# Low halves of the expert weights written over the pieces they are formed from

## The reference

```python
logits = (hf @ w_router + b_router).astype(jnp.float32)
top_vals, top_idx = lax.top_k(logits, TOP_EXPERTS)
gates = jax.nn.softmax(top_vals, axis=-1)
...
def expert_block(args):
    tok, g, e = args
    xb = h_pad[tok]
    gu = xb @ w_gu[e] + b_gu[e]
    glu = jnp.minimum(gu[:, :D_EXPERT], SWIGLU_LIMIT)
    lin = jnp.clip(gu[:, D_EXPERT:], -SWIGLU_LIMIT, SWIGLU_LIMIT)
    act = glu * jax.nn.sigmoid(SWIGLU_ALPHA * glu) * (lin + 1.0)
    return (act @ w_down[e] + b_down[e]) * g[:, None].astype(h.dtype)
```

## Time and profile before

| | us |
|---|---|
| median of 3 runs | 1449.99 |
| lowest and highest | 1448.58, 1451.81 |
| the profiled execution | 1450.44 |
| its span, first to last instruction | 1448.7 |

### The profile page before, as it was taken

How to read it: one execution, slowest core, us unless ns; L and a number is a source line. 1 busy time by engine, 2 the same in 40 slices (tenths; PEclk the granted TensorE clock), 3 DMA queues, 4 the chain that set the end, 5 groups by cost and what they waited for, 6 DMA issues and landing times. The chain is left out here.

```text
span 1448.7 us, 18694 instructions
## 1 busy us (share of the span) xinstructions
PE 1369.2 (95%) x6693; PEld 1112.4 (77%) x6696; DVE 1261.1 (87%) x1314; ACT 1117.4 (77%) x1221; POOL 220.0 (15%) x138
## 2 busy tenths in 40 slices
PE   6999878999999999999999999999999999999995
PEld 5887766786788878778777788787787787787884
DVE  5799778548899899999999899989999999998994
ACT  5666554455788898988988788988889888888783
POOL 1222000011111111211202011111111111030100
PEclk9999979999999999999999999999999999999998
DMA  5522011158999999999999999999999999999991
GB/s 152 148 71 73 30 59 45 45 193 307 332 382 376 371 379 398 405 389 396 395 401 386 395 374 401 406 388 393 387 389 397 381 391 379 400 391 385 378 391 30
DMA packets 85926, 448.52 MB, mean 310 GB/s; under 512 B 18496, under 2 KB 23616, under 8 KB 36608
## 3 DMA queue, kind: packets, MB, share of 16 engines
q1 hardware_dynamic: 73424, 428.32, 75.0%
q0 software_dynamic: 9792, 18.90, 5.4%
q10 hardware_dynamic: 2608, 0.01, 0.1%
HBM read 440.89 MB, written 23.07 MB: 320 GB/s over the span
## 5 line engine op out<-in xcount | busy, mean ns | idle before, releaser
L840 DVE TENSOR_TENSOR whl<-wraw,whl 128x2048 fp32r<-128x2048 f32 x384 | 864.3, 2286 | 70.8 <-ACT whl L835 68.6
L835 ACT ACTIVATE whl<-wraw 128x2048 fp32r<-128x2048 f32 x384 | 728.5, 1917 | 143.3 <-PE ps L2163 95.6
L2163 PE MATMUL ps<-whl,xT 128*128 128x512 f32 x2768 | 660.5, 394 | 8.4 <-DVE whl L840 3.9
L2163 PEld LDWEIGHTS ps<-whl,xT 128*128 128x128 f32 x2768 | 514.0, 188 | 124.8 <-DVE whl L840 14.8
L2163 PE MATMUL ps<-whl,aT 128*128 128x512 f32 x1312 | 314.1, 396 | 14.2 <-DVE whl L840 14.2
L2163 PEld LDWEIGHTS ps<-whl,aT 128*128 128x128 f32 x1312 | 245.2, 189 | 68.5 <-DVE whl L840 18.4
L1029 POOL DMA_INDIRECT out_dram<-ysb,idx x32 | 86.0, 2688 | 623.2 <-ACT ysb L1344 623.2
L1020 POOL DMA_INDIRECT xg<-h_rows,idx x32 | 84.7, 2648 | 258.8 <-DVE idx L1794 253.7
L1906 PE MATMUL ps<-W,HT 128*128 128x512 f32 (+1 forms) x184 | 72.1, 392 | 5.4 <-DVE W L612 4.4
L1908 PE MATMUL ps<-W,HT 128*128 128x512 f32 (+1 forms) x184 | 68.9, 375 | 0.0
L1907 PE MATMUL ps<-W,HT 128*128 128x512 f32 (+1 forms) x184 | 68.8, 374 | 0.0
(11 more groups left out here) (296 smaller groups left out, 1400.8 us busy)
## 6 DMA issues: line engine op xcount, KB each, us to landing
wraw<-in_w_gu_dram SPq DMA_DIRECT2D x256, 1024.0 KB, 15.8
wraw<-in_w_down_dram SPq DMA_DIRECT2D x128, 1024.0 KB, 14.5
WR<-in_w_in_dram SPq DMA_DIRECT2D x20, 512.0 KB, 3.7
WR<-in_w_o_dram SPq DMA_DIRECT2D x8, 512.0 KB, 3.7
xs<-in_x_dram SPq DMA_DIRECT2D x4, 512.0 KB, 7.7
WR<-in_x_dram SPq DMA_DIRECT2D x4, 512.0 KB, 3.8
out_dram<-WR SPq DMA_DIRECT2D x4, 512.0 KB, 3.3
h_rows<-WR SPq DMA_DIRECT2D x4, 512.0 KB, 2.6
```

The source lines that it names most:

```text
L835: act.activation(whl[:, n % HL, 0, :], wraw[n % RAW], ACT.Copy).then_inc(chunk_hi, 1)
L840: eng.tensor_tensor(whl[:, n % HL, 1, :], wraw[n % RAW], whl[:, n % HL, 0, :].bitcast(F32), ALU.subtract).then_inc(chunk_lo, 1)
L2163: ins = pe.matmul(bank, a[x_][j], w[:, b, j, 512 * q:512 * q + 512], start=c == NG and j == 0 and n == 0, stop=last and j == nj - 1 and n ...
```

## The change

The raw slots become ten and the upper halves six. The low half of a piece is written into its own raw slot, over the raw values, and read there by TensorE. The space is the same: six raw slots, two more where the first pair of halves lay, six upper halves of 8 KB behind them. As a raw slot now holds the low half until TensorE has used it, load n waits for `chunk_used` of piece n - 10, and upper half n for that of piece n - 6. The first eight loads are issued where they were; load 8 waits for the first upper half (after which `W1` is free), since slots 8 and 9 lie on `W1`. The number of landings of a slot in a round is no longer the same for each slot, as 384 isn't a multiple of 10, and `split_hi` counts them. `EARLY` keeps the first four upper halves where they stood.

```diff
--- before.py
+++ after.py
@@ -273,7 +273,8 @@
 NG, ND = KD, KD // 2
 NCH = NG + ND
 PER_ROUND = NCH * E
-RAW, HL = 8, 4
+RAW, HL = 10, 6
+PREFETCH, EARLY = 8, 4
 LEAD = 2
 GLU_TOP = LIMIT / (1.0 + math.exp(-ALPHA * LIMIT))
 DENSE_AT = [(0, 3), (0, NG), (1, 1), (1, 5)]
@@ -359,10 +360,12 @@
         x1T = xres.rearrange("p (k n) -> p k n", k=KD)
         GF = rel.rearrange("p a b -> p (a b)")
 
-        whl = place("whl", [P, HL, 2, 2048], F32R, offset=base + 49152)
+        whi = place("whi", [P, HL, 2048], F32R, offset=base + 65536)
         o_qb = base + 49152 + 65536
-        wraw = [place(f"wraw{s}", [P, 2048], F32, offset=base + 8192 * s if s < 6 else o_qb + 66560 + 8192 * (s - 6))
-                for s in range(RAW)]
+        slot_at = [base + 8192 * s if s < 6 else o_qb + 66560 + 8192 * (s - 6) if s < 8 else base + 8192 * (s - 2)
+                   for s in range(RAW)]
+        wraw = [place(f"wraw{s}", [P, 2048], F32, offset=slot_at[s]) for s in range(RAW)]
+        wlo = [place(f"wlo{s}", [P, 2048], F32R, offset=slot_at[s]) for s in range(RAW)]
         bgs = place("bgs", [P, 3072], F32R, offset=o_qb)
         bg_raw = place("bg_raw", [P, 3072], F32, offset=o_qb + 12288)
         aT = place("aT", [P, 2, KD, P], F32R, offset=o_qb + 16384)
@@ -823,22 +826,21 @@
         def load_chunk(eng, r, e, c, at_=None):
             n = chunk_no(e, c)
             w = wraw[n % RAW]
-            after(eng, chunk_lo, PER_ROUND * r + n - RAW + 1)
+            after(eng, chunk_used, PER_ROUND * r + max(n - RAW + 1, 0))
             eng.dma_start(w if c < NG else w.rearrange("p (j n) -> p j n", j=2),
                           chunk_src(e, c, at_)) \
                .then_inc(landed[n % RAW], 16)
 
         def split_hi(act, r, e, c):
             n = chunk_no(e, c)
-            act.wait_ge(landed[n % RAW], 16 * (PER_ROUND // RAW * r + n // RAW + 1))
+            act.wait_ge(landed[n % RAW], 16 * (len(range(n % RAW, PER_ROUND, RAW)) * r + n // RAW + 1))
             after(act, chunk_used, PER_ROUND * r + n - HL + 1)
-            act.activation(whl[:, n % HL, 0, :], wraw[n % RAW], ACT.Copy).then_inc(chunk_hi, 1)
+            act.activation(whi[:, n % HL, :], wraw[n % RAW], ACT.Copy).then_inc(chunk_hi, 1)
 
         def split_lo(eng, r, e, c):
             n = chunk_no(e, c)
             eng.wait_ge(chunk_hi, done(r, e, c))
-            eng.tensor_tensor(whl[:, n % HL, 1, :], wraw[n % RAW], whl[:, n % HL, 0, :].bitcast(F32),
-                              ALU.subtract).then_inc(chunk_lo, 1)
+            eng.tensor_tensor(wlo[n % RAW], wraw[n % RAW], whi[:, n % HL, :].bitcast(F32), ALU.subtract).then_inc(chunk_lo, 1)
 
         def most_of(eng):
 
@@ -914,7 +916,9 @@
                         if is0(r) and e == FIXED:
                             sp.wait_ge(ids_ok, 1)
                         ids_at[e] = sp.value_load(ids[0:1, e:e + 1], min_val=0, max_val=E - 1)
-                    if not is0(r) or chunk_no(e, c) >= RAW:
+                    if is0(r) and chunk_no(e, c) == PREFETCH:
+                        sp.wait_ge(chunk_hi, 1)
+                    if not is0(r) or chunk_no(e, c) >= PREFETCH:
                         load_chunk(sp, r, e, c, ids_at.get(e))
 
             stream(0)
@@ -1350,7 +1354,7 @@
                     split_hi(act, 0, 0, 2)
                     split_hi(act, 0, 0, 3)
                 turn_x_hi(r, 0)
-                for c in range(HL if is0(r) else 0, NG):
+                for c in range(EARLY if is0(r) else 0, NG):
                     split_hi(act, r, 0, c)
                     if is0(r) and c == 4:
                         turn_g_hi()
@@ -2154,13 +2158,14 @@
 
                 pe.wait_ge(chunk_lo, done(r, e, c))
                 nj = len(a[0])
-                w = whl[:, chunk_no(e, c) % HL].rearrange("p s (j n) -> p s j n", j=nj)
+                w = [half_.rearrange("p (j n) -> p j n", j=nj)
+                     for half_ in (whi[:, chunk_no(e, c) % HL, :], wlo[chunk_no(e, c) % RAW])]
                 last = c in (NG - 1, NCH - 1)
                 parts = ((0, 0), (0, 1)) if narrow(e) else ((0, 0), (0, 1), (1, 0))
                 for j in range(nj):
                     for n, (x_, b) in enumerate(parts):
                         for q, bank in enumerate(banks):
-                            ins = pe.matmul(bank, a[x_][j], w[:, b, j, 512 * q:512 * q + 512],
+                            ins = pe.matmul(bank, a[x_][j], w[b][:, j, 512 * q:512 * q + 512],
                                             start=c == NG and j == 0 and n == 0,
                                             stop=last and j == nj - 1 and n == len(parts) - 1)
                 ins.then_inc(chunk_used, 1)
```

## The result

The changed kernel is slower: 1455.07 us median (1451.28 to 1457.40, 20 runs) against 1450.80 (1447.59 to 1453.71, 20 runs) for the kernel before beside it; ratio 1.0029, 95% interval [1.0022, 1.0036].

A forecast was written before the change was run, and what follows sets the result against it. The DMA engines were taken to set the pace from about 540 us on, TensorE before. From 1450.4 us, -1.5 (tail) and -0.5 (early loads) gave 1448.4, and 0.4 less for the median 1448.0 us; range 1442 to 1454.

The forecast's parts named there:

- (4): At the start: loads 8 and 9 go out 11 us earlier, but products do not; 0 us.
- (5): Before the DMA queue fills near 530 us: shifted loads carry 1:1 to the end; -0.5 us, bounds -2.3 and +2.6.
- (1): VectorE's subtractions written in place: taken as nothing, at most 4.4 us of VectorE's 49 us of slack.
- (2): Loads waiting for TensorE's use of piece n - 10: up to 2.6 us later or some 2.3 us earlier.
- (3): Upper halves six pieces ahead: the last expert's clamp comes in time; -1.5 us, bounds 0 and -2.2.
- The early stretch loses: Between 350 and 530 us, shorter look-ahead and later loads fill the queue 6.4 us later; 1456 us, chance 0.14.
- The engines were the bound: In the bound stretch DMA has speed in reserve; the deeper lead removes TensorE's 22.1 us idle; 1428 us, chance 0.06.
- Early gain: Between 350 and 530 us, a fuller DMA queue wins back 6.4 us; 1442 us with the tail, chance 0.20.
- The signs: From 540 to 1300 us: DMA share 1.00, landing over 14 us, ScalarE waiting for DMA; last clamp starts with gate activation.

The follow-up runs named there:

- a1_hold: The changed kernel with load 8 and all later loads held until the first gather has landed; 1448.80 us, ratio 0.9989.
- b1_extra: The kernel before with two extra, unused 1 MB loads right behind load 7; 1457.37 us, ratio 1.0045.
- d1_one: The changed kernel with load 8 let out early but load 9 held until the first gather has landed; 1451.92 us, ratio 1.0013.
- c1_warm: The changed kernel with 40 instead of 20 idle products keeping TensorE at work before the first gather lands; 1452.40 us, ratio 1.0016.
- b2_hold67: The kernel before with loads 6 and 7 held until the first gather has landed; 1450.00 us, ratio 1.0000.
- a2_lead4: a1_hold with four upper halves used instead of six; 1448.48 us, ratio 0.9984.
- a4_hold67: a1_hold with loads 6 and 7 also held until the first gather has landed; 1449.67 us, ratio 0.9988.
- a1_repeat: a1_hold run once more, unaltered, against the kernel before; 1448.71 us, ratio 0.9987.
- a5_eight: a1_hold with eight slots for pieces instead of ten; 1457.36 us, ratio 1.0045.
- b3_halfdown: The kernel before, loading only the first half of each of the 128 down-projection pieces; 1436.10 us, ratio 0.9899.

## Why the prediction was wrong

**The step that failed is (4), the start, "Term: 0".** It got the issue times right (loads 8 and 9 follow load 7 at once) and asked only whether the two pieces are needed earlier. It did not ask what else is in the DMA engines at that time. The first gather is issued 3.5 us behind load 9, and TensorE waits for it: both traces show that wait, and the row for the kernel before was there to be read, 0.95 us of idle with the gather as releaser. The term is +5.2 us: 4.1 for the gather and 1.1 to 1.2 for the clock. With it the sum would have been 1448.0 + 5.2 = 1453.2 us, within 2 us of the median. a1_hold takes the term away, and its 1448.80 us show the rest of the sum to have been right within 1 us; b1_extra puts the term into the kernel before, d1_one halves its first part, c1_warm takes out its second.

**That it is carried 1:1** was in step (5) for shifts before the queue fills, and holds: +6.2 at piece 0, +6.0 at piece 344. Between piece 0 and some piece 66 TensorE is the limit and every load waits for a use, so loads shift with the products; behind it the DMA is the limit and starts late by as much. A single pair of traces strays by some 2 us on the way, though: b2_hold67 has -0.9 at piece 0 and -2.9 at piece 383.

**Step (1), the subtraction in place, nothing**: right. The group of the changed kernel has the mean of the earlier trace rows, 2286 ns:

```profile
L843 DVE TENSOR_TENSOR wlo<-wraw,whi 128x2048 fp32r<-128x2048 f32 x384 | 861.0, 2286 | 52.7 <-ACT whi L838 51.4
```

**Steps (2) and (5), ten slots tied to TensorE's use, -0.5 us**: with loads 8 and 9 held, two comparisons give 0.9989 and 0.9987, some 1.6 and 1.9 us less than the kernel before, upper bounds of the intervals 0.3 us. This gain of the whole change without the early loads is small and of the sign foretold, and near the 2.0 us that (3) and (5) had together. In its trace a1_hold goes from +1.0 us at piece 0 to 0.0 at piece 376 and loses the rest in the tail, but between them the shift moves by as much (-1.3 at piece 344). Which part of the change makes the gain is open: a1_hold and a2_lead4 share ten slots and the use-tied release, and a4_hold67 agrees with both; a run that alters only the release while the pairs stay would need space that is not there, and was not tried.

**Step (3), six upper halves, -1.5 us in the tail**: the mechanism is right and stands in the traces, at some 0.8 us; its worth in the time is not shown. In the last expert (kernel after):

```profile
1418.21 1.03 ACT L1337 ACTIVATE acts<-ps 128x1024 f32<-128x1024 f32 x1 [2.03 <-PE ps L2168]
1418.42 1.22 DVE L1829 TENSOR_SCALAR acts<-ps 128x1024 f32<-128x1024 f32 x1
```

The clamp starts 0.2 us behind the gate activation, as foretold, not 1.5 as in the earlier trace rows, and the shift falls there from +5.8 (piece 376) to +4.7 (piece 380), 1.1 us of the 1.5, of which 0.8 come at once behind the clamp, between pieces 377 and 378. That step of 0.8 is in the traces of all seven runs with six upper halves (after, a1_hold, a1_repeat, a4_hold67, a5_eight, c1_warm, d1_one) and in none of the four with four (a2_lead4, b1_extra, b2_hold67, b3_halfdown). But a2_lead4, without it, is as fast in the medians, and in its trace the clock gives back as much.

**The rivals.** "The early stretch loses" named 1456 us, 0.9 from the median, and as its point a landing of piece 66 more than 2 us behind; that landing did move, by 7.0 us. Yet its reason was not at work: piece 66 was late because everything since piece 0 was, and a1_hold, with the same slots, has it 1.7 us late and no loss. A time that fits doesn't prove a mechanism. a5_eight shows what that rival looks like when it is at work: uses unshifted, landings late. "The engines were the bound" is wrong, but less so than I had it: in b3_halfdown the time falls by only some 15 us when a sixth of the traffic goes. "Early gain" didn't come. My chance of 0.14 for slower was too low, since step (4) had been given no bound at all. Nor was 2.9 us the least that could be told from no change: the interval of the result is 1.0 us to either side.

**The signs.** DMA share 1.00, 273 loads, landing 16.4 us, ScalarE's waits gone from TensorE to DMA, the clamp with the gate activation: all right, and none of them touches what went wrong. SyncE's loads do wait for TensorE now (510 to 1300 us):

```profile
SPq L830 <- PE ps L2168: 636.6, 285, 6.3
```

## What to carry to other kernels

A load that is let out early, and costs nothing where it lands, can cost where it passes: list every transfer of every queue that is in the DMA engines between its new and its old time, and look whether an engine waits for one of them. Hold bulk loads behind the small gather that the first product needs (one wait, 6 us here: a1_hold beats both kernels). And where a stage is bound by a full queue for a thousand microseconds, any delay before it is paid in full at the end, so look at its first moments as hard as at its last.

## What the runs showed of the hardware

- The first gather (issue to landing) took 4.4 to 4.5 us with loads 6 and 7 ahead or with no load at all, 6.6 us with one more load of 1 MB ahead, 8.6 to 8.8 us with two. It landed with the last load issued ahead of it: 348.50 and 348.96 us (after), 346.62 and 346.45 (d1_one), 349.69 and 349.91 (c1_warm). The two kinds go through different queues, so I had not expected a gather to wait for nearly all of them. The packets tell in which part of its time. The kernel before, from the gather's issue to its landing (338.9 to 343.5 us):

```profile
q1 hardware_dynamic: 138, 0.97, 50.1%
q0 software_dynamic: 144, 0.30, 22.1%
```

  The changed kernel, 339.9 to 344.3 us, then 344.3 to 348.5 us:

```profile
q1 hardware_dynamic: 248, 1.88, 100.8%
```
```profile
q1 hardware_dynamic: 170, 1.13, 63.9%
q0 software_dynamic: 240, 0.39, 24.6%
```

  For 4.4 us after its issue no packet of the gather moves (4.2 in d1_one; 2.0 in the kernel before and in a1_hold), and from its first packet to its landing it takes 4.2 us (2.4 in d1_one, 2.5 in the kernel before and in a1_hold). So of the 4.1 us more, 2.4 pass before the first packet and 1.7 while packets of both queues move.

  The Trainium skill ("DMA: Bandwidth & Descriptors", section "Queues, rings and completion order") says that each DMA engine serves its queues in turn, a packet from each. By that, the gather's 144 packets, taking turns with as many load packets of 7.2 KB (1.88 + 1.13 MB in 248 + 170 packets), would let 144 x 7.2 KB, about 1 MB, pass, 2.4 us at 424 GB/s; this estimate falls short of the 4.1 us measured. For the second part the trace is near it, as 1.13 MB of loads moved there; for the first part it does not agree, as for 4.4 us the loads' queue alone was served. Why, no run here shows.

- A gap of TensorE of 3.07 us (d1_one), 5.03 us (after) or 5.22 us (b1_extra) was followed by a granted clock of 0.50 for 3.4, 3.4 and 6.8 us; one of 0.9 us (before, a1_hold, c1_warm) was not. The cost up to the use of piece 0 was 1.1 (after), 1.5 (d1_one) and 2.3 us (b1_extra). It does not follow every time: after 3.03 us without work near 1424 us the clock fell in the kernel before and stayed at 1.00 in a2_lead4.
